# Five norms of a deep hybrid block: the next product's first tile computed ahead of the norm

## The chip, the cores and the metric

The kernel runs on one core of a Trainium2 chip. The metric is the device time of one execution in microseconds (us). The engines are TensorE (PE, with PEld for its weight loads), VectorE (DVE), ScalarE (ACT), GpSimd (POOL) and SyncE (SP), which here issues the DMAs.

## The reference, cut to what matters

The reference computes a deep block on 512 tokens of width 1024: two layers, each of a SwiGLU feed-forward, a mixer and a second feed-forward, and then a second block of attention, RWKV and a feed-forward. Each sublayer begins with the same norm, scaled and shifted by modulation vectors that come from a condition `c`:

```
def rms_norm(x, g):
    xf = x.astype(jnp.float32)
    y = xf * lax.rsqrt(jnp.mean(xf * xf, axis=-1, keepdims=True) + EPS)
    return (y * g.astype(jnp.float32)).astype(x.dtype)

h = rms_norm(x, g) * (1 + scale) + shift
x = x + half * (1 + gate) * sublayer(h)
```

The next product is `h @ W`. Since the root of a token is one number, `h @ W` equals the root of the token times `(x * g * (1 + scale)) @ W`, plus `shift @ W`, which is one row for all tokens. At the end of the second layer there is a norm by `final_g` as well, and the second block's first norm is taken of its result.

## The kernel before

Activations lie transposed: 1024 channels as 8 chunks (`DC`) of 128 partitions, 512 tokens along the free dimension. `K.x` is the residual. Each product is done in three passes to keep float32 precision: the activation is split into `h_hi` and `h_lo`, a weight tile into `w_hi` and `w_lo`, and a chunk contributes `w_hi*h_hi`, `w_hi*h_lo` and `w_lo*h_hi` (L401 to L403), each a large product of 128x128 by 128x512 into one PSUM bank.

`gemm` (L270) runs over the output tiles of a product. A tile of weights is 128 output channels; its 8 chunks make 24 large products. In the projections back to the residual (`project`, L1050) an output block is made of two tiles: 11 chunks each in a feed-forward (33 large products a tile), 8 each in the mLSTM. SP loads raw weights into a ring of 4 slots. ACT makes `w_hi` (`split_hi`, L236) and DVE `w_lo` (`split_lo`, L243) in 2 halves, so the split of tile t+2 waits until tile t is done. The order of each engine's work is written out by hand: in a projection DVE first splits, then updates the residual from the bank (`dve_evac`, L1062), and ACT squares it (`Squares.by_act`, L544); POOL adds up the squares.

A norm lies between a projection and the next product. In `Modulated` (L636) TensorE sums the squares over the channels with one-column products (`sums_pe`, L605), ACT takes the root (L623), DVE the reciprocal (L628), and TensorE spreads it with four 128-column products to a bank with the row of roots for all tokens (`row_of_roots`, L598). Then DVE scales the eight chunks (L665), ACT adds the shift and rounds to `h_hi` (L652), and DVE takes the remainder `h_lo` (L668). Both engines split the weights of tile 1 between the root and the scaling. `first_pair` (L367) runs tiles 0 and 1 together: for each chunk, as it comes, the two products with `h_hi`, and at the end those with `h_lo` (L384).

There are seven such norms behind the first. Five are changed: the hybrid mixer's, that of the feed-forward "f10" (first of layer 1), the mLSTM's, that of "f11" (second of layer 1), and the final head in front of the second block (`FinalModulated`, L873). The final head has two roots: it sums two sets of squares, takes the first root, works out the second from it, and later has POOL multiply `K.x` itself by the first one. The norm behind the hybrid mixer ("f01") and the last in the second block stay as they are.

Behind a norm DVE has other work for each tile done: in the hybrid and the mLSTM four steps of a convolution (L1114, L1117), in f10 the accumulation of modulation vectors (L492, L495) and the gate's product, in f11 only the gate's product, in the second block two steps of a token shift (L2418, L2420).

## Time and profile before

| | |
|---|---|
| median of 3 runs | 3602.83 us (3602.04 to 3604.32) |
| profiled execution | 3600.31 us, span 3598.5 us |
| PE busy | 3466.9 us, 96% |
| DVE busy | 1980.1 us, 55% |
| ACT busy | 1183.8 us, 33% |
| POOL busy | 364.9 us, 10% |
| granted TensorE clock, mean | 0.973 of full speed |

A matmul's span in the profile overlaps that of the next one, so the time of a stream is read from the distances of starts. A clock of 1.00 is 2.4 GHz, 0.50 is 1.2 GHz. An operation's start counts from the beginning of the span. A float32 product of a narrow matrix appears as two instructions.

### The profile page before, as it was taken

The page shows a single profiled execution, that of the slowest core. Times are in us where ns is not written, and L with a number is a line of the kernel's source. Part 1 is how long each engine was busy: PE and PEld are TensorE (multiplying, and loading weights), DVE is VectorE, ACT ScalarE, POOL GpSimd, SP SyncE. Part 2 cuts the span into 40 slices and gives each one's busy share as a digit, 9 for nine tenths or more (in the row PEclk, how much of TensorE's full clock was granted, in tenths as well). Part 3 has the DMA queues.
Part 4 walks back from the last instruction along what each step waited for, and adds up shares of the span by engine and source line. Part 5 has one row for each costly group of instructions (what it writes and reads, how often), then busy time and mean ns, then how long its engine had stood idle before and what let it go on. Part 6 is the DMA issues. An engine that isn't in the chain of part 4 may idle for free. (4 is left out here: it accounts for less than half of the span.)

```text
span 3598.5 us, 56173 instructions
## 1 busy us (share of the span) xinstructions
PE 3466.9 (96%) x22376; PEld 2799.2 (78%) x22376; DVE 1980.1 (55%) x2770; ACT 1183.8 (33%) x1733; POOL 364.9 (10%) x264
## 2 busy tenths in 40 slices
PE   7999999999999999999999999999989999999998
PEld 4888777878888788876678788887768787878886
DVE  6665566756654666465343433355667773454343
ACT  3222245433222322233242322233434542233231
POOL 1000003410000000010101000130103330010000
PEclk9999999999999999999899999999989999989999
DMA  6555322125554555421032223222210002223332
GB/s 248 196 189 178 113 77 73 56 89 189 198 193 138 181 187 202 160 84 50 1 104 95 86 96 109 89 83 84 63 39 6 8 6 71 95 64 98 89 100 70
DMA packets 103764, 382.74 MB, mean 106 GB/s; under 512 B 11424, under 2 KB 15136, under 8 KB 103200
## 3 DMA queue, kind: packets, MB, share of 16 engines
q1 hardware_dynamic: 103584, 380.15, 31.4%
q8 instruction: 136, 2.23, 0.3%
q14 instruction: 44, 0.36, 0.0%
HBM read 378.01 MB, written 2.10 MB: 106 GB/s over the span
## 5 line engine op out<-in xcount | busy, mean ns | idle before, releaser
L401 PE MATMUL bank<-h_hi,w_hi 128*128 128x512 f32 x2616 | 1031.4, 394 | 20.3 <-DVE w_lo L246 17.5
L402 PE MATMUL bank<-h_lo,w_hi 128*128 128x512 f32 x2616 | 1021.8, 391 | 0.0
L403 PE MATMUL bank<-h_hi,w_lo 128*128 128x512 f32 x2616 | 1021.8, 391 | 0.0
L246 DVE TENSOR_TENSOR w_lo<-w_raw,w_hi 128x1024 fp32r<-128x1024 f32 (+2 forms) x480 | 645.9, 1346 | 512.4 <-ACT w_hi L240 502.6
L240 ACT ACTIVATE w_hi<-w_raw 128x1024 fp32r<-128x1024 f32 (+2 forms) x480 | 526.5, 1097 | 345.3 <-PE bank L403 283.5
L401 PEld LDWEIGHTS bank<-h_hi,w_hi 128*128 128x128 f32 x2616 | 493.2, 189 | 138.0 <-DVE w_lo L246 23.3
L403 PEld LDWEIGHTS bank<-h_hi,w_lo 128*128 128x128 f32 x2616 | 493.0, 188 | 104.3
L402 PEld LDWEIGHTS bank<-h_lo,w_hi 128*128 128x128 f32 x2616 | 493.5, 189 | 102.3 <-issue 1.9
L401 PE MATMUL bank<-f_gu_hi,w_hi 128*128 128x512 f32 x704 | 279.4, 397 | 0.0
L403 PE MATMUL bank<-f_gu_hi,w_lo 128*128 128x512 f32 x704 | 279.1, 396 | 0.0
L402 PE MATMUL bank<-f_gu_lo,w_hi 128*128 128x512 f32 x704 | 279.1, 396 | 0.0
L1020 ACT ACTIVATE f_gu_hi<-f_prod_t 128x512 f32 (+1 forms) x88 | 55.6, 632 | 408.0 <-DVE f_prod_t L1027 408.0
L495 DVE SCALAR_TENSOR_TENSOR ada_acc<-ada_tiles,c_act,ada_acc 128x512 f32<-128x512 f32 x210 | 157.5, 750 | 7.2 <-DMA ada_tiles<-in_ada 1.4
L401 PEld LDWEIGHTS bank<-f_gu_hi,w_hi 128*128 128x128 f32 x704 | 132.6, 188 | 32.6
L403 PEld LDWEIGHTS bank<-f_gu_hi,w_lo 128*128 128x128 f32 x704 | 132.6, 188 | 32.4
L402 PEld LDWEIGHTS bank<-f_gu_lo,w_hi 128*128 128x128 f32 x704 | 132.6, 188 | 32.2
L1027 DVE TENSOR_TENSOR f_prod_t<-f_sil_t,bank 128x512 f32<-128x512 f32 x88 | 60.5, 688 | 167.7 <-PE bank L403 167.7
L1017 ACT ACTIVATE f_sil_t<-bank 128x512 f32<-128x512 f32 x88 | 52.7, 599 | 245.7 <-PE bank L403 245.6
L1066 DVE SCALAR_TENSOR_TENSOR residual<-bank,coef,residual 128x512 f32 (+1 forms) x40 | 30.0, 751 | 166.3 <-PE bank L403 166.3
L542 POOL MEMSET sq_acc_f<- 128x512 f32 x5 | 2.6, 526 | 1037.6 <-PE bank L403 1037.6
L1029 DVE TENSOR_TENSOR f_gu_lo<-f_prod_t,f_gu_hi 128x512 f32 (+1 forms) x88 | 60.9, 692 | 77.9 <-ACT f_gu_hi L1020 77.9
L402 PE MATMUL bank<-u_lo,w_hi 128*128 128x512 f32 x256 | 101.5, 396 | 0.0
(618 smaller groups left out, 4604.8 us busy)
## 6 DMA issues: line engine op xcount, KB each, us to landing
ada_tiles<-in_ada SPq DMA_DIRECT2D x180, 512.0 KB, 4.1
w_raw<-in_gu SPq DMA_DIRECT2D x176, 512.0 KB, 4.4
w_raw<-in_dn SPq DMA_DIRECT2D x64, 704.0 KB, 4.2
w_raw<-in_w_ff SPq DMA_DIRECT2D x64, 512.0 KB, 3.6
w_raw<-in_w_hyb SPq DMA_DIRECT2D x36, 512.0 KB, 3.4
w_raw<-in_w_rkv SPq DMA_DIRECT2D x24, 512.0 KB, 3.5
w_raw<-in_w_attn SPq DMA_DIRECT2D x20, 512.0 KB, 3.6
w_raw<-in_w_hout SPq DMA_DIRECT2D x16, 512.0 KB, 3.4
```

The lines of the kernel that those rows point to most:

```text
L240: K.nc.scalar.activation(K.w_hi[:, half, 0:kb * P], K.w_raw[:, slot, 0:kb * P], ACT.Copy).then_inc(K.hi_done.sem, 1)
L246: K.nc.vector.tensor_tensor(K.w_lo[:, half, 0:kb * P], K.w_raw[:, slot, 0:kb * P], K.w_hi[:, half, 0:kb * P].bitcast(F32), ALU.subtract).t ...
L401: nc.tensor.matmul(K.ps[bank][:], wh, hi, start=start, stop=False)
L402: nc.tensor.matmul(K.ps[bank][:], wh, lo, start=False, stop=False)
L403: last_mm = nc.tensor.matmul(K.ps[bank][:], wl, hi, start=False, stop=stop)
L495: ins = v.scalar_tensor_tensor(self.acc[:], block, c, self.acc[:], ALU.mult, ALU.add)
L542: self.K.nc.gpsimd.memset(acc[:], 0.0).then_inc(self.K.sq_added.sem, 1)
L1017: nc.scalar.activation(sil[:, j // 2, :], K.ps[j][:], ACT.Silu).then_inc(sil_done.sem, 1)
L1020: nc.scalar.activation(gu_hi[:, bass.ds(f, 1), :], prod[:, j // 2:j // 2 + 1, :], ACT.Copy).then_inc(guhi_done.sem, 1)
L1027: nc.vector.tensor_tensor(prod[:, j // 2, :], sil[:, j // 2, :], K.ps[j][:], ALU.mult).then_inc(done.sem, 1)
L1029: nc.vector.tensor_tensor(gu_lo[:, bass.ds(f, 1), :], prod[:, j // 2:j // 2 + 1, :], gu_hi[:, bass.ds(f, 1), :].bitcast(F32), ALU.subtract ...
L1066: nc.vector.scalar_tensor_tensor(K.x[:, bass.ds(o, 1), :], K.ps[j // tpo][:, None, :], K.coef[:, bass.ds(o, 1)], K.x[:, bass.ds(o, 1), :], ...
```

## The change

Five norms get `early=True`, and the projection in front of each gets the coming norm as `follow`.

In the projection, each output block of the residual is multiplied by the norm's gain times (1 + scale) as soon as it is updated, and split into `h_hi` and `h_lo`, without the root and the shift: one operation more on ACT (`ahead_act`) and one on DVE (`ahead_dve`) per block. For this the gain is computed at the start of the projection (`gain_ahead`), and the squares' tiles move to memory that the projection's predecessor has left (`vacated`).

In the next product, TensorE runs tile 0 in full at once on these (`early_tile`). Between its 24 large products stand the narrow ones, one at a time (`between`): the 8 sums of squares (16 in the final head), the 4 products of the row of roots (behind the tile in the final head), and 8 new products `shift @ W` of the raw weights with the shift. The true `h` is then made as before, with the scaling of chunk c waiting until the early tile has read it. When it is done, tile 0's bank is copied to memory by ACT, multiplied by the row of roots by DVE, and the shift's column is added by ACT; only then does the tile count as done. Tiles 1 and 2 are run one behind the other with `h_hi`, then with `h_lo` (`next_pair`), instead of tiles 0 and 1 chunk by chunk; the weights of tile 2 are split within the norm (`third_weights`), between chunks 3 and 4 on ACT and between scaling and `h_lo` on DVE. SP holds its loads of later weight tiles until the shift's products are done. Some semaphores are shared with other stages to make room.

```diff
+            if early:
+                sp.wait_ge(K.early_mm.sem, K.early_mm(1))
...
+            def early_tile():
+                pe.wait_ge(K.lo_done.sem, g0 + PRIMED + 1)
+                pe_wait(pe, 0, 0, 0)
+                pe.wait_ge(K.bank_free.sem, K.bank_free(-1))
+                for n in range(3 * kb):
+                    c, part = n // 3, n % 3
+                    hi, lo, bank, start, stop = mm(c, 0)
+                    wh, wl = weights(0, c)
+                    if part == 0:
+                        pe.wait_ge(K.h_ready.sem, K.h_ready(c + 1 - kb))
+                        nc.tensor.matmul(K.ps[bank][:], wh, hi, start=start, stop=False)
+                    elif part == 1:
+                        nc.tensor.matmul(K.ps[bank][:], wh, lo, start=False, stop=False)
+                    else:
+                        nc.tensor.matmul(K.ps[bank][:], wl, hi, start=False, stop=stop).then_inc(K.early_read.sem, 1)
+                    head.between(pe, n)
+                head.behind(pe)
+
+            def next_pair():
+                for j in (1, 2):
+                    pe.wait_ge(K.lo_done.sem, g0 + j + PRIMED + 1)
+                    pe_wait(pe, 0, j, j)
+                    for k in range(kb):
+                        pe.wait_ge(K.h_hi_done.sem, K.h_hi_done(k + 1))
+                        hi, lo, bank, start, stop = mm(k, j)
+                        wh, wl = weights(j, k)
+                        nc.tensor.matmul(K.ps[bank][:], wh, hi, start=start, stop=False)
+                        nc.tensor.matmul(K.ps[bank][:], wl, hi, start=False, stop=False)
+                pe.wait_ge(K.tile_mm.sem, done0 + 1)
+                for j in (1, 2):
+                    for k in range(kb):
+                        hi, lo, bank, start, stop = mm(k, j)
+                        pe.wait_ge(K.h_ready.sem, K.h_ready(k + 1))
+                        last_mm = nc.tensor.matmul(K.ps[bank][:], weights(j, k)[0], lo, start=False, stop=stop)
+                    last_mm.then_inc(K.tile_mm.sem, 1)
...
+    def ahead_act(self, act, o):
+        K.nc.scalar.activation(K.h_hi[:, bass.ds(o, 1), :], K.x[:, bass.ds(o, 1), :], ACT.Identity, scale=K.gain[:, bass.ds(o, 1)]).then_inc(K.h_hi_done.sem, 1)
+    def ahead_dve(self, dve, o):
+        dve.wait_ge(K.h_hi_done.sem, K.h_hi_done(o + 1))
+        K.nc.vector.scalar_tensor_tensor(K.h_lo[:, bass.ds(o, 1), :], K.x[:, bass.ds(o, 1), :], K.gain[:, bass.ds(o, 1)],
+                                         K.h_hi[:, bass.ds(o, 1), :].bitcast(F32), ALU.mult, ALU.subtract).then_inc(K.h_ready.sem, 1)
...
+    def between(self, pe, n):
+        if 2 <= n < 2 + 2 * NT:
+            self.sum_part(pe, n - 2)
+        if 13 <= n < 13 + NT:
+            self.row_part(pe, n - 13)
+        if n >= 2 * DC:
+            self.shift_part(pe, n - 2 * DC)
...
+    def early_act(self, act, second_weights, third_weights):
+        second_weights()
+        self.rms_act(act)
+        for c in range(DC):
+            act.wait_ge(K.scaled.sem, K.scaled(c + 1))
+            K.nc.scalar.activation(K.h_hi[:, c, :], K.t[:, c, :], ACT.Identity, bias=self.shift[:, c:c + 1]).then_inc(K.h_hi_done.sem, 1)
+            if c == 3:
+                third_weights()
+        K.nc.scalar.activation(K.early_tile, self.in_halves(K.ps[0]), ACT.Copy).then_inc(K.early_copied.sem, 1)
+        act.wait_ge(K.early_fixed.sem, K.early_fixed(2))
+        K.nc.scalar.activation(K.ps[0][:], K.ps[0][:], ACT.Identity, bias=K.early_bias[:, 0:1]).then_inc(K.tile_mm.sem, 1)
...
+    def early_dve(self, dve, second_weights, third_weights):
+        second_weights()
+        self.rms_dve(dve)
+        dve.wait_ge(K.rms_row.sem, K.rms_row(1))
+        for c in range(DC):
+            dve.wait_ge(K.early_read.sem, K.early_read(c + 1))
+            v.scalar_tensor_tensor(K.t[:, c, :], K.x[:, c, :], K.gain[:, c:c + 1], K.ps[self.ROW][:], ALU.mult, ALU.mult).then_inc(K.scaled.sem, 1)
+        third_weights()
+        self.bias(dve)
+        for c in range(DC):
+            dve.wait_ge(K.h_hi_done.sem, K.h_hi_done(c + 1))
+            v.scalar_tensor_tensor(K.h_lo[:, c, :], K.t[:, c, :], self.shift[:, c:c + 1], K.h_hi[:, c, :].bitcast(F32),
+                                   ALU.add, ALU.subtract).then_inc(K.h_ready.sem, 1)
+            if c == 1:
+                dve.wait_ge(K.early_copied.sem, K.early_copied(1))
+                v.tensor_tensor(self.in_halves(K.ps[0]), K.early_tile, self.in_halves(K.ps[self.ROW]), ALU.mult).then_inc(K.early_fixed.sem, 1)
...
 class FinalModulated(Modulated):
+    def between(self, pe, n):
+        if 1 <= n < 1 + 4 * NT:
+            self.sum_part(pe, n - 1)
+        if n >= 2 * DC:
+            self.shift_part(pe, n - 2 * DC)
+    def behind(self, pe):
+        self.row_of_roots(pe)
...
         v.reciprocal(K.rs[:], K.rs[:]).then_inc(self.own_r, 1)
+        self.copy_bias(dve)
         dve.wait_ge(self.own_r, 4)
         v.tensor_tensor(K.rs[:], K.rs[:], self.r[:], ALU.mult).then_inc(K.rms_step.sem, 1)
...
+            if follow:
+                follow.ahead_dve(dve, o)
```

## Rows read from the trace of the kernel before

**Rows 1.** The page, busy time of each engine and instructions.
```profile
PE 3466.9 (96%) x22376; PEld 2799.2 (78%) x22376; DVE 1980.1 (55%) x2770; ACT 1183.8 (33%) x1733; POOL 364.9 (10%) x264
```

**Rows 2.** TensorE's waits: us in total, times, longest us.
```profile
PE bank L401 <- DVE w_lo L246: 18.8, 22, 4.5
```

**Rows 3.** Windows, five norms: us; busy PE, PEld, DVE, ACT, POOL; clock; DMA.
```profile
411.29:433.16 21.87, 18.55 (x82) 14.85 (x80) 14.30 (x23) 9.27 (x14) 0.00 (x0) 0.77 0.31 100
1168.93:1190.80 21.87, 18.56 (x83) 14.80 (x81) 14.34 (x23) 9.52 (x14) 0.00 (x0) 0.77 0.20 73
1544.44:1566.28 21.84, 18.53 (x82) 14.84 (x80) 15.27 (x25) 9.52 (x14) 8.39 (x7) 0.77 0.27 89
1983.10:2003.81 20.71, 16.75 (x75) 13.51 (x73) 14.12 (x21) 9.52 (x14) 0.00 (x0) 0.84 0.08 26
2355.89:2378.73 22.84, 19.84 (x99) 16.89 (x97) 15.09 (x28) 10.71 (x17) 6.89 (x3) 0.85 0.16 47
```

**Rows 4.** Windows in and behind the hybrid's norm.
```profile
418.99:424.00 5.01, 5.01 (x12) 3.95 (x13) 5.01 (x9) 4.46 (x7) 0.00 (x0) 0.50 0.22 86
...
433.16:444.30 11.14, 11.14 (x49) 9.19 (x50) 10.50 (x14) 2.73 (x5) 0.00 (x0) 1.00 0.29 94
```

**Rows 5.** Timeline of the hybrid's norm: start, us, engine, line, operation.
```profile
411.73 0.75 DVE L1066 SCALAR_TENSOR_TENSOR residual<-bank,coef,residual 128x512 f32<-128x512 f32 x1 [4.01 <-PE bank L403]
...
412.51 0.63 ACT L547 ACTIVATE sq_f<-residual 128x512 f32<-128x512 f32 x1 [5.88 <-DVE residual L1066]
...
413.19 1.38 PE L617 MATMUL bank<-consts,sq_f 128*128 128x1 f32 x8 [0.33 <-ACT sq_f L547]
414.61 0.26 ACT L623 ACTIVATE rms_rs<-bank,cols 128x4 f32<-128x4 f32 x1 [1.47 <-PE bank L617]
414.77 1.05 ACT L240 ACTIVATE w_hi<-w_raw 128x1024 fp32r<-128x1024 f32 x1
...
415.14 2.07 PE L602 MATMUL bank<-consts,rms_rs 128*128 128x128 f32 x8 [0.57 <-DVE rms_rs L628]
...
417.34 5.36 DVE L665 SCALAR_TENSOR_TENSOR h_scaled<-residual,gain,bank 128x512 f32<-128x512 f32 x8 [0.26 <-PE bank L602]
418.12 5.33 ACT L652 ACTIVATE h_hi<-h_scaled,mods 128x512 fp32r<-128x512 f32 x8 [2.30 <-DVE h_scaled L665]
...
418.99 0.77 PE L378 MATMUL bank<-h_hi,w_hi 128*128 128x512 f32 x1 [1.77 <-ACT h_hi L652]
...
422.61 5.38 DVE L668 SCALAR_TENSOR_TENSOR h_lo<-h_scaled,mods,h_hi 128x512 fp32r<-128x512 f32 x8
```

**Rows 6.** Timeline of TensorE, a batch of narrow products between large ones.
```profile
712.70 1.84 PE L1618 MATMUL bank<-consts,ssd_acc 128*128 128x1 f32 x16
714.40 0.47 PE L401 MATMUL bank<-hyb_hi,w_hi 128*128 128x512 f32 x1
```

**Rows 7.** Timeline of DVE behind the hybrid's norm.
```profile
435.99 1.22 DVE L246 TENSOR_TENSOR w_lo<-w_raw,w_hi 128x1024 fp32r<-128x1024 f32 x1
437.13 0.55 DVE L1114 TENSOR_SCALAR proj<-conv_raw,cols 128x512 f32<-128x512 f32 x1
...
439.95 0.54 DVE L1114 TENSOR_SCALAR proj<-conv_raw,cols 128x512 f32<-128x512 f32 x1
```

**Rows 8.** Timeline of DVE behind the norm of f10.
```profile
1191.17 2.39 DVE L495 SCALAR_TENSOR_TENSOR ada_acc<-ada_tiles,c_turn,ada_acc 128x512 f32<-128x512 f32 x3
...
1199.44 0.75 DVE L495 SCALAR_TENSOR_TENSOR ada_acc<-ada_tiles,c_turn,ada_acc 128x512 f32<-128x512 f32 x1 [1.30 <-DMA ada_tiles<-in_ada]
```

**Rows 9.** Timeline of DVE in a feed-forward's and the mLSTM's projection.
```profile
1156.62 2.10 DVE L246 TENSOR_TENSOR w_lo<-w_raw,w_hi 128x1408 fp32r<-128x1408 f32 x1 [0.53 <-ACT w_hi L240]
...
1974.69 1.47 DVE L246 TENSOR_TENSOR w_lo<-w_raw,w_hi 128x1024 fp32r<-128x1024 f32 x1 [1.65 <-ACT w_hi L240]
```

**Rows 10.** Timeline of DVE in the final head.
```profile
2362.60 0.16 DVE L911 TENSOR_TENSOR rms_rs<-rms_rs,final_r 128x4 f32<-128x4 f32 x1
...
2365.00 5.36 DVE L665 SCALAR_TENSOR_TENSOR h_scaled<-residual,gain,bank 128x512 f32<-128x512 f32 x8 [0.37 <-PE bank L602]
```

More of the change, by code:

```diff
@@ L278, in gemm @@
     done0 = g0 + PRIMED
+    early = head and head.early
     with one_block(K) as block:
@@ L316, in body @@
                     if head and isinstance(i, int) and t < 3:
-                        if t < 2:
+                        if t < 2 and not (early and t == 0):
                             split_hi(K, act, kb, (t + 2) % RING, t % SPLIT, g0 + t + 2)
@@ L343, in body @@
                     if head and isinstance(i, int) and t < 3:
-                        if t < 2:
+                        if t < 2 and not (early and t == 0):
                             split_lo(K, dve, kb, (t + 2) % RING, t % SPLIT, g0 + t + 2)
@@ L362, in _ @@
         def _(pe):
-            if head:
+            if head and not early:
                 head.pe(pe)
@@ L389, in body @@
                     t = turn * i + j
-                    if head and isinstance(i, int) and t < 2:
+                    if early and isinstance(i, int) and t < 3:
+                        if t == 0:
+                            early_tile()
+                        if t == 1:
+                            next_pair()
+                    elif head and isinstance(i, int) and t < 2:
                         if t == 0:
@@ L588 @@
     SUM, ROW = 4, 5
+    early = False
     def __init__(self, K):
@@ L636, with __init__, gain_ahead @@
 class Modulated(Rms):
-    def __init__(self, K, gain, scale, shift):
+    SHIFT_BANK = 6
+    def __init__(self, K, gain, scale, shift, early=False):
         super().__init__(K)
-        self.gain, self.scale, self.shift = gain, scale, shift
+        self.gain, self.scale, self.shift, self.early = gain, scale, shift, early
+    def gain_ahead(self, dve):
+        K = self.K
+        dve.wait_ge(K.x_written.sem, K.x_written(0))
+        K.nc.vector.scalar_tensor_tensor(K.gain[:], self.scale, 1.0, self.gain, ALU.add, ALU.mult).then_inc(K.x_written.sem, 1)
+        dve.wait_ge(K.x_written.sem, K.x_written(1))
@@ new lines, in ahead_advance, with sum_part @@
+    def ahead_advance(self):
+        K = self.K
+        K.x_written.base += self.GAIN_STEPS
+        K.h_hi_done.base += DC
+        K.h_ready.base += DC
+    def sum_part(self, pe, i):
+        K, mm = self.K, self.K.nc.tensor.matmul
+        total, half = K.ps[self.SUM], NT * len(K.sq_parts)
+        a, t = i % half, i % NT
+        acc, end = K.sq_parts[a // NT]
+        if i == 0:
+            pe.wait_ge(K.sq_added.sem, K.sq_added(0))
+        if i == half:
+            pe.wait_ge(K.sq_done.sem, K.sq_done(0))
+        last = mm(total[:, a:a + 1], (acc if i < half else end)[:, t * P:(t + 1) * P], K.ones[:, 0:1], start=i == 0, stop=i >= half, skip_group_check=True)
+        if i == 2 * half - 1:
+            last.then_inc(K.rms_sum.sem, 1)
@@ new lines, in row_part, with shift_part @@
+    def row_part(self, pe, t):
+        K = self.K
+        if t == 0:
+            pe.wait_ge(K.rms_step.sem, K.rms_step(1))
+        last = K.nc.tensor.matmul(K.ps[self.ROW][:, t * P:(t + 1) * P], K.rs[:, t:t + 1].to_broadcast([P, P]), K.ident, start=True, stop=True)
+        if t == NT - 1:
+            last.then_inc(K.rms_row.sem, 1)
+    def shift_part(self, pe, c):
+        K = self.K
+        last = K.nc.tensor.matmul(K.ps[self.SHIFT_BANK][:, 0:1], K.w_raw[:, 0, c * P:(c + 1) * P], self.shift[:, c:c + 1], start=c == 0, stop=c == DC - 1)
+        if c == DC - 1:
+            last.then_inc(K.early_mm.sem, 1)
@@ L672, in advance @@
         self.rms_advance()
-        self.K.x_written.base += 1
+        if self.early:
+            for c, n in ((self.K.early_mm, 1), (self.K.early_read, DC), (self.K.early_copied, 1), (self.K.early_fixed, 2)):
+                c.base += n
+        else:
+            self.K.x_written.base += 1
         for c in (self.K.scaled, self.K.h_hi_done, self.K.h_ready):
@@ L878, in __init__ @@
     def __init__(self, K, gain, scale, shift, final, row):
-        super().__init__(K, gain, scale, shift)
+        super().__init__(K, gain, scale, shift, early=True)
         self.final, self.row = final, row
@@ L882, in __init__, with bias, gain_ahead, behind @@
         self.r, self.both = K.final_small
-    def pe(self, pe):
+    GAIN_STEPS = 2
+    def between(self, pe, n):
[3 more added lines that the diff above has]
+            self.shift_part(pe, n - 2 * DC)
+    def bias(self, dve):
+        pass
+    def gain_ahead(self, dve):
+        super().gain_ahead(dve)
+        K = self.K
+        K.nc.vector.tensor_tensor(K.gain[:], K.gain[:], self.final, ALU.mult).then_inc(K.x_written.sem, 1)
+        dve.wait_ge(K.x_written.sem, K.x_written(2))
+    def behind(self, pe):
         K, mm = self.K, self.K.nc.tensor.matmul
-        self.rms_pe(pe)
+        self.row_of_roots(pe)
         for t in range(NT):
@@ L1047, in root_table, with project @@
     K.nc.scalar.activation(K.pad4[:], K.consts[:, 0:NT], ACT.Sqrt)
-def project(K, w, kb, tpo, mm, nxt, gate, half, squares, turn=4, side=None, ready=None):
+def project(K, w, kb, tpo, mm, nxt, gate, half, squares, turn=4, side=None, ready=None, follow=None):
     nc = K.nc
@@ L2185, in ml_heads, with final_head, second_block @@
     return out, N["spr"].sem
-def second_block(K):
+def final_head(K):
+    row = K.at("final_row", [P, S], F32, K.arena + 100 * 1024)
+    return FinalModulated(K, col(K, "mix_pre", 0, 8), K.mods[:, 152:160], K.mods[:, 144:152], col(K, "final_g", 0, 8), row)
+def second_block(K, head):
     nc, d = K.nc, K.dram
@@ L3527, in build @@
                 with stage(K):
-                    mlstm(K, nxt, head, gate)
+                    mlstm(K, nxt, head, gate, follow)
             else:
```

116 lines of the change are left out of this document (81 added, 35 removed).

## The prediction

> **What bounds the kernel now.** I read the page first: TensorE is busy for 96% of the span [rows 1], so time can only be saved where its stream of large products breaks or slows. The list of TensorE's waits came next: the largest sum is 18.8 us in 22 short waits for a weight's remainder `w_lo`, no more than 4.5 us at a place [rows 2]; no steady stage is starved. Then I laid one window over each norm that changes, from the start of the projection's last large product to the start of the third tile (tile 2) of the next product: 21.87, 21.87, 21.84, 20.71 and 22.84 us [rows 3]. Two tiles are done in each, 48 large products. A full-speed stretch shows 11.14 us for 48 of them, 0.232 each [rows 4]. So the five windows hold 109.1 us where 55.7 us would do: some 53 us are all that the change can touch, in the order hybrid, FFN 10, mLSTM, FFN 11, final head. Last I read the timeline of the first of them engine by engine [rows 5]. It is a chain: residual update 411.73, square 412.51, sums 413.19, root 414.61, row of roots 415.14, scaling 417.34, `h_hi` 418.12, first large product 418.99. The granted clock is at its half level (1.2 GHz) from inside the gap until 424.0, and products there take 0.42 us [rows 4].
>
> **Part by part: the early tile.** I walk the hybrid's norm on the profile's clock. The last large product starts at 411.29, the modulation's narrow products stay, and the early tile starts at 411.80. ACT does the last square at 412.51; the last chunk's early `h_hi` starts at 413.05, its `h_lo` on DVE at 413.79 (a back-to-back ACT operation follows after 0.54 to 0.66, a dependent one after 0.78) [rows 5]. The tile needs that chunk only in its 22nd product, so it doesn't wait.
>
> **The narrow products.** A float32 narrow product is two instructions. In a batch between large ones 16 of them take 712.70 to 714.40, 0.106 each [rows 6], so 0.213 a product. No row shows one singly between large products. Bounds: nothing (its loads hide behind the large one) and 0.43 (the half-clock pitch of the rows of roots, 2.07 us for 8 instructions) [rows 5]. I take 0.213, since the batch is the nearest row: one load hides, two don't.
> The Trainium skill (TensorE: Matmul & The Clock Gate, "What happens when you issue a matmul") says that the queue pulls weight loads ahead of matmuls in flight. By it alone the single products would be nearly free; the batch's 0.106 an instruction doesn't show that.
> Eight sums then stand between products 2 to 9, each pair 0.44, and end at 415.6 instead of 414.3. ACT's root goes to about 415.95, the reciprocal to 416.25; DVE has by then done the split of tile 1, which moved ahead of the root. TensorE takes the four row products from 416.7 to 418.2. The scaling starts at 418.55, 1.2 us LATER than the 417.34 of before. The eight shift products (new, 1.7 us) and the rest of the tile end at 421.55.
>
> **Behind it.** DVE is now the long queue. Scaling takes 5.27 us (417.34 to 422.61) [rows 5], to 423.8; the split of tile 2, newly put here, 1.14 (435.99 to 437.13) [rows 7]; the bias copy 0.2; eight `h_lo` 5.28 (0.66 each); the product with the row of roots in the bank 0.69: to 431.1. ACT fits in: four `h_hi`, the split of tile 2 (1.05, as the row of tile 1 [rows 5]), four more to 425.7, the bank's copy, the bias, to about 427.9. TensorE does tiles 1 and 2 from 421.6, waits some 1 us for `h_hi` behind the inserted split, and ends both at 433.5, at full clock.
> Tile 3 needs a split on DVE, and behind `h_lo` stands the work of the tiles already done. In the hybrid that is 2.8 to 2.9 us of convolution a tile (437.13 to 439.95) [rows 7]: evacuation 0 to 434.0, split to 435.2, evacuations 1 and 2 to 440.85, split of tile 4 to 442.1. Tile 4 starts at 442.2. Before it starts at 433.16 + 11.14 = 444.3. **Hybrid: 2.1 us won**, not the 7.5 us gap. The mLSTM's norm has the same convolution and 21.84 for 21.87: **2.1**.
> FFN 10 has four modulation steps there, 2.9 us (2.39 for three); tile 4 waits for the modulation's data, whose load is issued behind the fourth step (ending at 1193.5) and is first used at 1199.44 [rows 8]. That step ends 24.5 us after the last large product before, 22.7 in the new walk: **1.9**.
> FFN 11 has no such work, so TensorE sets the end. Before, tile 3 starts 20.71 + 5.57 = 26.3 us after the last large product; new, without the 0.3 us of modulation's narrow products, 434.3 - 411.3 - 0.3 = 22.7: **3.6**.
> The final head has 16 sums, between products 1 to 16. They end at about 2363.2; 2.3 us later than before. Then DVE copies the bias in the middle of the chain of roots, and this waits for the last shift product, that is for the end of the early tile: 2366.7. The roots step ends at 2367.3, where it began at 2362.60, and scaling starts at 2368.5 instead of 2365.00 [rows 10]. TensorE idles 0.7 and 1.0 us around the rows. Tile 3 starts at 2384.6, before at 2378.73 + 5.57 = 2384.3: **0.3 lost**.
>
> **The projections ahead.** Each output block gets one ACT operation (0.65) and one on DVE (0.75), some 40 of each. They stand before the split of the weights of the tile after next. In the mLSTM's projection, the shortest tile (24 products, 5.6 us), the split of `w_lo` runs from 1974.69 to 1976.16 [rows 9], and is wanted at 1977.5. Put 0.67 later, and less slowed by the squares' addition beside it, it ends at about 1976.8. In the FFN's the split of before ends at 1158.7 [rows 9]; the early `h_lo` and two modulation steps move it to at most 1160.3, with the tile boundary at 1161.2. So nothing is paid. If the cover goes: up to 0.7 us an output, 8 outputs, five projections, 28 us; I hold nearly all of it off.
> The gain's column moves to the projection's start (0.2 us on DVE, under a tile of 7.7 us), the cleared accumulators wait for a semaphore long up, both zero. SP now holds the loads of tiles 4 and 5 until the early tile's shift products are done (421.5 instead of 412.85 and 417): they land some 4 us later, and tile 4 is split no earlier than 434. SP's modulation loads stand behind the same wait but are due later. Zero; without the cover, a tile's load of 4 us.
>
> **Sum.** 2.1 + 1.9 + 2.1 + 3.6 - 0.3 = 9.4 us. The profiled execution took 3600.31 us (span 3598.5), which gives 3590.9; it stands 2.5 under the median of the runs, 3602.83, so the forecast is **3593.5**. The bounds of the narrow price move the scaling by about 1.0 us earlier (then ACT's and DVE's splits hold the root) or 2.6 us later, in four norms, three of them bound by DVE: 3589.5 (1.0 in four) to 3604 (2.6 in four).
>
> **Rivals.**
> A. The single narrow products are nearly free, and the final head's chain is hardly later than now. The pitch in [rows 6] speaks against. Scaling 1.0 us earlier in four norms, and about 1.5 in the head: 3593.5 - 5.5 = 3588.
> B. The queue on DVE (scaling, split, `h_lo`, evacuations) eats the whole early tile, or the added operations in the projections cost 0.2 us a block where a split ran close. Against: the slack worked out above, for: DVE's unbroken run of splits and evacuations, of the kind in [rows 7], with some 20 us of work ahead of it. 9.4 less about 8: 3601.5.
> C, the other side. The granted clock drops during the early tile, because every second instruction is narrow. For it: it fell in all five windows (means 0.77 to 0.85) [rows 3], while sums and rows ran. Against: large products pass in between in at least half of that time. Price: products at 0.42 instead of 0.232 over some 7 to 10 us (18 products, 3.4 us), the narrow ones at 0.43 push the scaling by 1.5 or more; 4.9 us in four norms, DVE's queue not hiding it: 3593.5 + 20 = 3613. It decides from about half of the norms on. In the head alone, where TensorE idles twice, a half clock would cost up to 2 us; that is in my range.
>
> **Chances.** Forecast 0.58, A 0.14, B 0.18, C 0.10. A change under 0.2% (7.2 us) can't be told from none. The forecast's own range, 3589.5 to 3597.5, is faster by over 0.2% in about 0.8 of its part; with A that makes 0.60 faster; B and the rest 0.29 same; C and a little of B 0.11 slower. Range: 3586 to 3604.
>
> **What would show it.** Right: the first large product of the next weights starts about 0.5 us behind the last of the projection; scaling in the hybrid starts 7.3 us behind that last product (6.05 now); granted clock 1.00 through the first four windows; last product to tile 4's start 30.9 us in the hybrid (33.0 now), FFN 11 to tile 3 22.7 (26.3 now), the head unchanged. The single narrow product's price can be read as the pitch of large ones around it less 0.232. Wrong: half clock inside the windows (C), `w_lo` waits inside the projections (B), pitches near 0.24 around narrow ones (A).

## The result, with the profile after

The changed kernel took 3579.07 us (median of four runs, 3575.18 to 3582.20), the kernel before 3603.57 beside it (3602.04 to 3608.23): ratio 0.9929, 95% interval 0.9912 to 0.9947. Gained are 24.5 us; 9.4 were forecast (3593.5 us), and the time lies under the range, 3586 to 3604. The profiled execution took 3580.06 us with a span of 3578.2, that is 20.3 less than the span of before.

The page's busy line [rows 1 of before], then the longest sum of TensorE's waits [rows 2]:

```profile
PE 3448.2 (96%) x22456; PEld 2780.9 (78%) x22456; DVE 2018.7 (56%) x2820; ACT 1212.7 (34%) x1783; POOL 360.7 (10%) x264
```
```profile
PE bank L457 <- DVE w_lo L252: 27.8, 28, 4.5
```

TensorE has 80 instructions more and is busy 18.7 us less: what it won is speed, not only gaps. The waits for `w_lo` rose from 18.8 to 27.8 us, so part of each norm's gain turned into that wait. Windows of the changed kernel over the same five places, from the last large product to the 49th behind it (the start of the third tile before; in the changed kernel the same amount of work is done by then, but tiles 1 and 2 both lack products), columns as in [rows 3]:

```profile
410.82:427.62 16.80, 16.80 (x98) 13.47 (x97) 12.33 (x20) 9.82 (x16) 0.00 (x0) 1.00 0.46 161
1166.49:1183.29 16.80, 16.80 (x99) 13.46 (x97) 12.34 (x20) 9.84 (x16) 0.00 (x0) 1.00 0.26 96
1538.76:1555.56 16.80, 16.80 (x99) 13.46 (x97) 12.74 (x22) 9.83 (x16) 7.62 (x7) 1.00 0.41 147
1964.33:1980.74 16.41, 16.41 (x91) 13.38 (x89) 12.24 (x19) 9.84 (x16) 0.00 (x0) 1.00 0.27 96
2333.16:2355.22 22.06, 20.12 (x114) 15.98 (x113) 12.97 (x24) 10.83 (x18) 0.00 (x0) 1.00 0.22 69
```

TensorE is busy from end to end in four of them, and the granted clock is 1.00 in all. Against 109.1 us of before they take 88.9, so 20.2 us are won at this point. More than half of that is given back on DVE. Its timeline behind the hybrid's norm (start, us, line, operation; answers to [rows 5] and [rows 7]):

```profile
418.28 5.36 DVE L799 SCALAR_TENSOR_TENSOR h_scaled<-residual,gain,bank 128x512 f32<-128x512 f32 x8 [2.16 <-PE bank L747]
423.55 1.22 DVE L252 TENSOR_TENSOR w_lo<-w_raw,w_hi 128x1024 fp32r<-128x1024 f32 x1
...
426.68 4.06 DVE L804 SCALAR_TENSOR_TENSOR h_lo<-h_scaled,mods,h_hi 128x512 fp32r<-128x512 f32 x6
...
430.80 0.55 DVE L1312 TENSOR_SCALAR proj<-conv_raw,cols 128x512 f32<-128x512 f32 x1
431.38 2.33 DVE L1315 SCALAR_TENSOR_TENSOR proj<-conv_raw,cols,proj 128x512 f32<-128x512 f32 x3
433.62 1.22 DVE L252 TENSOR_TENSOR w_lo<-w_raw,w_hi 128x1024 fp32r<-128x1024 f32 x1
...
440.39 1.22 DVE L252 TENSOR_TENSOR w_lo<-w_raw,w_hi 128x1024 fp32r<-128x1024 f32 x1
```

From 423.55 on DVE hardly rests, and tile 4 of the weights (the fifth) waits for the split of 440.39: it starts at 441.67, 30.85 us behind the last large product, where 30.9 were forecast.

The distances from a projection's last large product to the start of tile 3 and of tile 4, worked out from the starts of products in each trace:

```
                hybrid      FFN 10      mLSTM       FFN 11      head
before          27.47/32.91 27.46/33.33 27.46/32.90 26.28/31.72 28.42/33.86
after           24.07/30.85 23.93/30.75 23.92/30.78 22.66/28.26 29.10/35.33
saved, tile 4   2.06        2.58        2.12        3.46        -1.47
```

That is 8.75 us. Where the rest of the span's 20.3 lies: start to the first norm 0.5; stretches between norms -0.1, 0.7 and 0.5; behind the head -1.0; **from the mLSTM's norm to FFN 11's 11.0**. Nearly all of these 11.0 are in the mLSTM's four heads, whose instructions the change doesn't touch. Windows from one head's denominators (20 one-column products) to the next's, three periods, first of the kernel before, then of the changed one:

```profile
1678.80:1712.90 34.10, 33.29 (x142) 22.75 (x142) 11.14 (x29) 9.22 (x22) 5.49 (x7) 0.90 0.00 0
1712.90:1747.00 34.10, 33.31 (x143) 22.70 (x143) 14.43 (x34) 10.50 (x23) 5.50 (x7) 0.90 0.00 1
1747.00:1781.10 34.10, 33.32 (x143) 22.65 (x143) 14.43 (x34) 10.50 (x23) 5.50 (x7) 0.90 0.00 0
```
```profile
1671.70:1704.10 32.40, 31.65 (x142) 21.27 (x142) 11.11 (x29) 9.21 (x22) 5.49 (x7) 0.95 0.00 1
1704.10:1734.90 30.80, 29.99 (x143) 20.58 (x143) 14.45 (x34) 10.50 (x23) 5.50 (x7) 1.00 0.00 1
1734.90:1765.60 30.70, 29.92 (x143) 20.50 (x143) 14.36 (x34) 10.50 (x23) 5.50 (x7) 1.00 0.00 1
```

The same instructions; the granted clock is 0.90 in the one and, from the second head on, 1.00 in the other. Before, it fell to half (1.2 GHz) in each head. TensorE waits 0.8 us for the exponentials (`mlh_e`; 2.2 in the first head), runs 20 one-column products, and the large ones behind them start at half clock. The two rows and a window of the kernel before:

```profile
1678.84 3.31 PE L1962 MATMUL bank<-consts,mlh_e 128*128 128x1 f32 x20 [2.16 <-DVE mlh_e L2122]
...
1712.91 3.25 PE L1962 MATMUL bank<-consts,mlh_e 128*128 128x1 f32 x20 [0.78 <-DVE mlh_e L2122]
```
```profile
1714.20:1721.00 6.80, 6.80 (x19) 4.75 (x20) 3.48 (x9) 0.33 (x1) 0.00 (x0) 0.50 0.01 4
```

One such fall costs 3.4 us a head (34.1 for 30.7). A run of heads that take 34.1 us each is called stuck below, one of heads at 30.7 free.

### The profile page after: what moved, and what is told of

Same layout as the page of the kernel before. It is cut to its first block and busy times, and to the rows that moved or that the text cites. A ratio compares the mean times of both kernels' runs of the same rounds, so it can differ in the third digit from the quotient of the medians.

```text
span 3578.2 us, 56582 instructions
## 1 busy us (share of the span) xinstructions
PE 3448.2 (96%) x22456; PEld 2780.9 (78%) x22456; DVE 2018.7 (56%) x2820; ACT 1212.7 (34%) x1783; POOL 360.7 (10%) x264
## 3 DMA queue, kind: packets, MB, share of 16 engines
q1 hardware_dynamic: 103584, 380.15, 30.7%
## 5 line engine op out<-in xcount | busy, mean ns | idle before, releaser
L457 PE MATMUL bank<-h_hi,w_hi 128*128 128x512 f32 x2576 | 1015.5, 394 | 29.2 <-DVE w_lo L252 26.5
L459 PE MATMUL bank<-h_hi,w_lo 128*128 128x512 f32 x2576 | 1005.6, 390 | 0.0
L458 PE MATMUL bank<-h_lo,w_hi 128*128 128x512 f32 x2576 | 1005.3, 390 | 0.0
L252 DVE TENSOR_TENSOR w_lo<-w_raw,w_hi 128x1024 fp32r<-128x1024 f32 (+2 forms) x480 | 634.3, 1321 | 397.7 <-ACT w_hi L246 386.5
L457 PEld LDWEIGHTS bank<-h_hi,w_hi 128*128 128x128 f32 x2576 | 485.3, 188 | 146.5 <-DVE w_lo L252 30.0
L459 PEld LDWEIGHTS bank<-h_hi,w_lo 128*128 128x128 f32 x2576 | 485.0, 188 | 102.4
L458 PEld LDWEIGHTS bank<-h_lo,w_hi 128*128 128x128 f32 x2576 | 485.5, 188 | 100.7 <-issue 1.9
L457 PEld LDWEIGHTS bank<-f_gu_hi,w_hi 128*128 128x128 f32 x704 | 132.2, 188 | 32.4
L459 PE MATMUL bank<-u_hi,w_lo 128*128 128x512 f32 x256 | 100.9, 394 | 0.0
```

The source lines that it names most:

```text
L252: K.nc.vector.tensor_tensor(K.w_lo[:, half, 0:kb * P], K.w_raw[:, slot, 0:kb * P], K.w_hi[:, half, 0:kb * P].bitcast(F32), ALU.subtract).t ...
L457: nc.tensor.matmul(K.ps[bank][:], wh, hi, start=start, stop=False)
L458: nc.tensor.matmul(K.ps[bank][:], wh, lo, start=False, stop=False)
L459: last_mm = nc.tensor.matmul(K.ps[bank][:], wl, hi, start=False, stop=stop)
```

## The experiments

All but three single executions were timed beside the kernel before. Three questions: is it the clock in the heads, what decides it, and are the norms' terms right.

**Are the kernels' times one group?** The kernel before again, no edit.

> The kernel before, unchanged, for a second trace. Theory H (the changed kernel won some 11 us in the mLSTM heads only because its heads meet the clock's steps at another offset, each head's pause no longer falling to the half clock): the half clock appears in all four heads again, as in the first trace (five stretches of 6.8 us between 1680 and 1806), and the time is 3602 to 3608. If the offset were drawn anew in each execution, the number of half-clock stretches in the heads would differ from the first trace and single times would scatter by some 10 us. Rival R (the shared semaphores or the shorter code of the heads make them faster): the same time, nothing said on the clock.

Measured: 3606.05 us (3593.42 to 3608.98, 10 runs), ratio 0.9997 (0.9983 to 1.0011). Heads 34.08 a period, as before. The distances of the norms in its trace are those of before to 0.3 us.

**Do shared semaphores hold the heads?** The change let `mlh_` counts share the hybrid's semaphores; this edit does that alone.

```
-    N = {n: K.count("mlh_" + n) for n in names}
+    N = {n: Count(K.hybrid_then_ml[n]) if n in K.hybrid_then_ml else K.count("mlh_" + n) for n in names}
```

> The kernel before with only the change's sharing of six semaphores between the hybrid mixer and the mLSTM heads. Rival R: the heads go from about 200 us to 189 us, total about 3592. Theory H: within 2 us of the kernel before, 3602 to 3606, half clock in all heads.

Measured: 3606.62 us (3598.16 to 3610.02), ratio 1.0004 (0.9991 to 1.0017), heads unchanged. The rival is refuted.

**Does the moment of arrival decide?** N idle large products into a bank that nobody reads, in the mLSTM's projection, ahead of the heads: 13, 6, then 4.

```
+    def pads(pe, t):
+        if isinstance(t, int) and t == 12:
+            for n in range(4):
+                nc.tensor.matmul(K.ps[6][:], K.h_hi[:, 0, 0:P], K.h_hi[:, 0, :], start=True, stop=True)
```

> The kernel before with 13 idle large products (3.0 us) on TensorE behind the 13th tile of the mLSTM's up product, ahead of the heads. Their results go to a bank that nobody reads. [...] Theory H: the heads fall to the half clock less often, some 11 us less in them, total 3603.6 + 3.0 - 11 = 3596. Rival R: 3603.6 + 3.0 = 3606.6.

> The same with 6 idle products (1.4 us). Theory H: the heads take some time between that of the kernel before and 11 us less, and it goes with the number of half-clock stretches in them at about 3.3 us a stretch of 6.8; total 3594 to 3605. Rival R: 3605.0, heads as before.

> The kernel before with 4 idle large products (0.9 us) on TensorE ahead of the mLSTM heads. In five traces of kernels of the kind before, the first head began 1.6 to 2.2 us behind a step of the clock where nothing was added; this makes it 2.5 to 3.1. Theory H2: that is among the free offsets (2.98 with 6 products was free): period of the heads 30.7 us, not 34.1, and most times lower by some 9 us: median about 3597. Rival R: no effect of an idle product, 3607 and heads of 34.1 us.

Measured: 13: 3605.20 us (3598.74 to 3611.74), where 3596 were expected; the profiled execution had heads of 34.09 a period. 6: 3605.53 us, five runs at 3598.1 to 3602.7 and five at 3608.4 to 3611.5; its profiled execution is of the lower five and has free heads (30.73). Neither moved the median (ratios 0.9996 and 1.0007). 4: **3596.07 us** (3592.86 to 3600.09, 10 runs), ratio 0.9970 (0.9961 to 0.9980): 0.9 us of useless work made the kernel before 11.1 us faster than the 3607.21 beside it. The three periods with 4:

```profile
1678.80:1712.80 34.00, 33.23 (x142) 22.89 (x142) 11.13 (x29) 9.22 (x22) 5.50 (x7) 0.90 0.00 0
1712.80:1743.50 30.70, 29.95 (x142) 20.54 (x142) 14.37 (x34) 10.51 (x23) 5.50 (x7) 1.00 0.00 1
1743.50:1774.30 30.80, 29.97 (x143) 20.55 (x143) 14.47 (x34) 10.51 (x23) 5.50 (x7) 1.00 0.00 1
```

From the second head on the clock stays full, as in the changed kernel. So the 11 us belong to no instruction of the change: they can be had without it.

**The changed kernel again.** Unaltered on two chips, and with 4 and 8 idle products.

> The changed kernel, unchanged, for a second trace and more times. Theory H2 (as H, with a cause for the offset: in the kernel before each norm ends inside a half-clock stretch, and its end moves only about half as far as its beginning against the clock's steps, so that seven norms pull all executions to nearly the same offset at the heads, mostly one in which each head falls; with the norms at full clock nothing pulls any more, and the heads are met at all offsets): the time scatters in two groups, about 3576 to 3585 with the heads free and about 3588 to 3598 with them at half clock, more in the first; median 3580 to 3590 against 3606 before. Rival R2 (the heads are freed by the change itself, always): all times within 3575 to 3584.

> The changed kernel unaltered, on another chip. If the offset at the heads decides and the changed kernel reaches them at more than one offset, its times spread from about 3577 to 3596, the heads in its trace 237 to 239 us where the profiled execution is of the faster part and 245 or more where it is of the slower; median 3584 to 3590, 15 to 20 us under the kernel before.

> The changed kernel with 4 idle large products (0.9 us) on TensorE ahead of the mLSTM heads, as before_pad4 had them. In three traces of the changed kernel the first head began 0.86 to 1.00 us behind a step of the clock, and the heads were free. Theory H2: 1.8 us is among the offsets at which each head falls (1.64 to 2.15 did): heads at a period of 34.1 us, times about 3595 to 3599, so the same idle products that took 11 us from the kernel before now add 10 in those executions that were fast. Rival (TensorE's idle products help in themselves, say by their activity): 3583 or less.

> The same with 8 idle products (1.8 us). Theory H2: 2.7 to 2.8 us, among the free offsets (2.57 to 2.98 were): period 30.7 us in the trace, few or no times in the slow group; median 3584 to 3588, under the 3593.9 that the changed kernel gave in the last call. Rival as above: nothing more than the 4 products gave.

Measured: again 3593.88 us (3581.85 to 3596.10, 7 runs), ratio 0.9960 (0.9946 to 0.9974); third 3583.66 (3581.50 to 3593.64, 6 runs), 0.9946 (0.9929 to 0.9962); pad 4 3591.73 (3581.50 to 3593.78, 4 runs); pad 8 3582.30 (3580.04 to 3591.68, 4 runs). The same 4 idle products that freed the heads of the kernel before left those of the changed kernel stuck in its trace (34.09), and 8 left them free (30.73): it is not the added work as such that helps. The changed kernel, unaltered, has two groups: of its 17 executions 11 took 3575.2 to 3586.3 us (mean 3581.7) and 6 took 3593.4 to 3596.1 (mean 3594.3), none between. The third's profiled execution is of the upper group, and has the half clock in its heads:

```profile
1672.20:1704.60 32.40, 31.64 (x142) 21.45 (x142) 11.11 (x29) 9.22 (x22) 5.50 (x7) 0.95 0.00 1
1704.60:1738.70 34.10, 33.29 (x142) 22.76 (x142) 14.43 (x34) 10.50 (x23) 5.50 (x7) 0.90 0.00 1
...
```

The moments at which the granted clock changes in a trace all stand on one even grid. The offset of a head is its start less the last point of that grid. Where the pauses were left as they are, the second and third heads that took 34.1 us began at offsets of 1.48 to 2.18 us, and those that took 30.7 at 2.24 to 2.90, whichever kernel it was (16 traces, those of the later experiments included). There is a third form: heads of 32.4 us, with half as long a stretch of half clock, at 1.46, 1.47 and 3.17. So in these traces the offset alone tells what a head takes. Two heads of the third form, from the kernel with the plain head below:

```profile
1707.80:1740.20 32.40, 31.63 (x142) 21.48 (x142) 14.37 (x34) 10.51 (x23) 5.50 (x7) 0.95 0.00 1
1740.20:1772.60 32.40, 31.64 (x142) 21.38 (x142) 14.38 (x34) 10.51 (x23) 5.50 (x7) 0.95 0.00 1
```

A period of 34.1 us carries a head to nearly the same offset again (2.15, 2.10, 2.03, 1.98 in the kernel before), and so does one of 30.7 (2.71, 2.72, 2.73 in the changed one). That is why an execution mostly stays as it began. It need not: the offset of stuck heads falls by 0.03 to 0.07 us a head, and one trace (narrow products in batches, below) went from 1.49 to 1.46 and so to 32.4.

**Parts of the change.** Without FFN 11's early tile; without the hybrid's.

```
-            elif step != "hyb":
+            elif step not in ("hyb", "ml"):      # the other kernel: ("hyb", "f00")
```

> The changed kernel with the norm of f11 alone as before. It lies behind the heads. From the last large product of the mLSTM's projection to the start of tile 3: 26.3 us instead of the 22.4 or so of the changed kernel, the half clock back in this norm, everything else unchanged: 3.6 us to 3.9 us more there. Rival to the walk (the early tile's worth is not that of the norm but of the clock behind it): under 2 us.

> The changed kernel with the hybrid mixer's norm alone as before. From the last large product to the start of tile 4: 33.0 us instead of 30.85, 2.1 us more; the half clock back in this norm. Theory H2: the heads take 237 or 248 us as the offset falls, which one run can't foretell.

Measured: 3586.76 us and 3596.74 (one run each). In the traces FFN 11's distance to tile 3 goes to 26.13 (3.5 more, 3.6 to 3.9 expected) and to tile 4 to 31.57 (3.3 more), the hybrid's to tile 4 to 32.98 (2.1 more); the others stay within 0.2. So these two norms pay for themselves. The second kernel's heads were stuck (34.1): its 3596.74 tells of that and not of the hybrid.

**The head as before, with 8 idle products**, meant as a better kernel, since the early tile had cost 1.5 us there.

```
-    super().__init__(K, gain, scale, shift, early=True)
+    super().__init__(K, gain, scale, shift)
```

> The candidate: the changed kernel with the 8 idle products, and the final head's norm as before, since it measured 1.5 us later at tile 4 with the change. Last large product to the start of tile 4 33.9 us there instead of 35.3. By that 1.5 us under after_pad8: 3583 to 3587. Rival: the final head's new order also keeps the clock up behind it; then no gain or a loss of up to 3 us.

Measured: 3596.66 us (3586.86 to 3603.28, 10 runs), ratio 0.9972. It failed, for two reasons that its trace shows. The mLSTM's heads took 34.1, 32.4 and 32.4 us, against 34.1, 30.7 and 30.7 in the trace with 8 idle products and the early head. And the plain head took 37.59 us to tile 4, the early one 35.33. With the early head the distance is 35.32 to 35.34 in all eleven traces. With the plain one it is 33.86 and 33.76 in the two traces of the unedited kernel before and 35.98 to 37.59 in all seven traces of kernels that have an edit elsewhere. So the early head loses 1.5 us against the unedited kernel, and gains 0.7 to 2.3 against the edited ones. Why an edit elsewhere changes the plain head isn't shown; how it does stands in the last section.

**Narrow products in batches.** All eight sums behind the sixth large product, four rows behind another, the shifts behind the last.

```
-        if 2 <= n < 2 + 2 * NT:
-            self.sum_part(pe, n - 2)
+        if n == 5:
+            for i in range(2 * NT):
+                self.sum_part(pe, i)
```

> The changed kernel with its narrow products in batches in four norms (8 sums behind the 6th large product, 4 rows behind the 14th, 8 shift products behind the last) instead of one at a time; the final head stays. By the walk a narrow product costs 0.213 us between large ones either way (measured 0.225 singly): last large product of the projection to the start of tile 4 in the hybrid's norm 30.85 us, within 0.5. Rival (singly is what makes it work: batches let the clock drop or wait on the chain): over 1 us later, half clock in the norm.

> The changed kernel with its narrow products in batches again: eight sums behind one large product, four row products behind another, eight shifts behind a third. Theory (a lone narrow product costs 0.22 us of TensorE, one within a batch 0.11): tiles 3 come 0.7 us earlier in the hybrid, mLSTM and f11 norms, tile 4 0.46 later in f10; about 1.7 us faster than the changed kernel, lost in the two groups of times, so between 3578 and 3592. Rival (singly is better, since the large products hide them): 2 to 4 us slower.

Timelines of the hybrid's early tile, TensorE, first singly, then in batches:

```profile
412.14 0.28 PE L739 MATMUL bank<-consts,sq_acc_f 128*128 128x1 f32 x2
412.27 0.48 PE L412 MATMUL bank<-h_hi,w_hi 128*128 128x512 f32 x1
412.59 0.28 PE L739 MATMUL bank<-consts,sq_acc_f 128*128 128x1 f32 x2
...
415.33 0.28 PE L739 MATMUL bank<-consts,sq_f 128*128 128x1 f32 x2
415.47 0.48 PE L414 MATMUL bank<-h_lo,w_hi 128*128 128x512 f32 x1
...
421.39 0.48 PE L428 MATMUL bank<-h_hi,w_hi 128*128 128x512 f32 x1
```
```profile
411.62 0.95 PE L739 MATMUL bank<-consts,sq_acc_f 128*128 128x1 f32 x8
412.43 1.03 PE L739 MATMUL bank<-consts,sq_f 128*128 128x1 f32 x8
413.32 0.49 PE L412 MATMUL bank<-h_hi,w_hi 128*128 128x512 f32 x1
...
420.15 0.49 PE L428 MATMUL bank<-h_hi,w_hi 128*128 128x512 f32 x1
```

Singly a narrow product costs 412.59 - 412.14 - 0.232 = 0.22 us, in the batch (413.32 - 411.62) / 8 = 0.21. (The 0.11 of the second expectation is the price of one of its two instructions, and wrong for a product.) The tile takes as long either way: 10.06 and 10.03 us. But the batch's last sum starts 3.0 us behind the tile's start, and the single ones' 4.0, so scaling starts 6.75 us behind the last large product and not 7.46. Tiles 3 come 0.7 us earlier. Time: 3584.91 us (3578.99 to 3593.81, 6 runs) and 3585.78 (one run). A gain of 1.7 us can't be seen between groups that stand 12 us apart; by the traces batches are the better form.

**Work in the heads' pauses.** Seven idle large products between the denominators of each head, then eighteen, in both kernels.

```
                         last = mm(K.ps[4][:, t:t + 1], e_of(sb, (t - sb) * P, P), K.ones[:, 0:1], start=sb == 0, stop=sb == t)
+                        if (t, sb) != (3, 3):
+                            for _ in range(2): mm(K.ps[5][:], K.h_hi[:, 0, 0:P], K.h_hi[:, 0, :], start=True, stop=True)
```

> The kernel before with seven idle large products per head between the narrow den products of the mLSTM heads (into a bank that nobody reads). Theory (the half clock in the heads' pauses makes the two groups of times): the granted clock stays 1.00 in the heads, a head takes 30.73 us plus 7 x 0.227 = 1.6, so 32.3 us and not 34.1, the four heads take about 3.4 x 4 less and 6.4 us more; time about 3598 and one narrow group. Rival (something else makes them): 6.4 us slower than the kernel before, about 3612, with two groups 10 us apart as before.

> The changed kernel with the same seven idle products per head. Theory: one narrow group, about 3588; against before_fill 9 to 10 us faster, which is what the norms alone save (8.9 us by their distances in the traces), and not 24. Rival (the change itself saves the time in the heads): the distance to before_fill stays near 20 us, and after_fill is 6.4 us slower than the changed kernel.

> The kernel before with eighteen idle large products per head, two behind each narrow den product but the last. Theory (the half clock belongs to the pause with little work): no half clock in the heads, period 30.73 + 18 x 0.233 = 34.9 us, heads 4.2 x 4 = 16.8 us longer than the free ones and 3.4 longer than the stuck ones; about 3609. Rival (the waits ahead of the den products alone, some 1 us, pull the clock down whatever follows): half clock as before in some heads, 38 us for such a head, 3615 and more.

> The changed kernel with the same eighteen. Theory: the heads as in before_full to 0.5 us, time about 3599, 9 to 10 us under before_full. Rival (a part of the gain lies in the rest of the kernel): 14 to 16 us under before_full, as between the kernels with seven.

Measured with seven: 3607.70 (3597.77 to 3615.44) and 3592.05 (3586.05 to 3596.00), 12 runs each. The clock still fell in the first and third pause of both traces (periods 37.2, 32.4, 35.6 and 35.7, 32.4, 35.7): the remedy was too weak. The changed kernel's times closed to one group of 10 us, the other's still spread over 18. With eighteen: 3616.44 (3612.74 to 3623.99, 6 runs) and 3602.83 (3599.84 to 3607.95, 12 runs). The first two periods with eighteen, kernel before, then changed:

```profile
1678.20:1717.90 39.70, 38.92 (x161) 27.72 (x161) 11.18 (x29) 9.23 (x22) 5.50 (x7) 0.87 0.00 0
1717.90:1752.80 34.90, 34.12 (x161) 23.93 (x161) 14.40 (x34) 10.51 (x23) 5.50 (x7) 1.00 0.00 1
...
```
```profile
1676.20:1715.90 39.70, 38.95 (x160) 27.45 (x160) 11.11 (x29) 9.22 (x22) 5.49 (x7) 0.87 0.00 1
1715.90:1750.80 34.90, 34.13 (x160) 23.94 (x160) 14.39 (x34) 10.51 (x23) 5.50 (x7) 1.00 0.00 1
...
```

From the second head on the clock is full in both, and the period is the 34.9 us worked out ahead; the first head fell, after its longer wait. The heads are now the same in both kernels (109.5 us for three periods), and what is left between them is 13.6 us; with seven it is 15.7. Each has about 6 us of uncertainty (from the intervals of the ratios).

**Putting it together.** Mean over the traces of each kind, the norms' distances to tile 4 add up to 166.0 us before (eight traces) and 156.0 after (seven with all five early tiles and single narrow products): 1.7, 2.0, 1.9, 4.0 and 0.3, **9.9 us**. In the unedited kernels alone they are 164.7 (two traces) and 156.1 (three), 8.5 us; the head makes most of the difference. The stretches ahead of and between the norms, without that of the mLSTM's heads, give 1.3 more (2.1 in the unedited kernels). A part of the heads' gain is there in either state: the first head took 34.1 us in the unedited kernel before and 32.4 in the changed one, stuck or free behind it, and the stretch from the mLSTM's norm to FFN 11's is 405.8 and 405.9 us in the two traces of the kernel before and 404.4 in the stuck one of the changed kernel. That is another 1.4. Together it makes 12.0 to 12.6. With eighteen products in the pauses the heads are alike, the 1.4 doesn't count, and 11.2 stand against 13.6.

Within a group it is much the same: of all 114 executions of the kernel before 17 lie under 3600 (mean 3595.1), 13.5 above the changed one's lower group, and 97 over it (mean 3606.2), 11.8 above its upper group. The rest of the gain is the mix: 15% of executions in the lower group before, 65% after. The means (3604.5 and 3586.1) stand 18.4 us apart: 12.5 within the groups and 6 by the mix. The first measurement, 24.5, had four executions of the lower group against four of the upper. No unedited execution of the kernel before in its lower group was traced; that its heads run free there is inferred from the traces with 4 and 6 idle products.

**Open.** The offset of the first head was 1.67 to 2.15 us in four of five traces of the kernel before without idle products ahead of the heads (0.11 in the fifth); behind an unfilled pause that leaves the second head stuck. In six such traces with the early norms it was 0.48 to 1.21. Of those six the two with filled pauses don't bear on the next step; in the other four the first head took 32.4 us and brought the second to 2.18 (stuck) once and to 2.57 to 2.71 (free) three times. The two traces with batches stand outside this: their first heads began at 3.31 and 1.55, and the second was stuck in both. Why each kernel arrives where it does is not shown, and the theory of the expectation for the changed kernel's repeat, that half-clock norms pull all executions to one offset, was not tested. Without the hybrid's early tile the first head began at 0.02 and the second stuck; without FFN 11's, which comes behind the heads, nothing changed there. That agrees with arrival as the cause and proves no rule. The stretch from the head's tile 4 to the end varied from 1207.1 to 1215.2 us over all traces, with no difference between the kinds (1211.1 and 1210.7 in the mean).

## Why the prediction failed, by its own steps

- *"some 53 us are all that the change can touch"*: **this is the step that failed.** It took every stretch outside the five windows to keep its time. The heads' stretch became 11.0 us shorter although no instruction there changed, because their pauses let the clock fall to half or not by the moment at which they begin (offsets of 1.48 to 2.18 and of 2.24 to 2.90 us), and every norm ahead of them had moved that moment. No rival had it: C looked for a half clock inside the early tile only. The trace of before held the sign, equal periods of 34.1 us with a granted clock of 0.90 in a stage whose pause is 0.8 us, and I did not open it, since the diff doesn't touch it.
- *The early tile.* Right: 411.33 for 411.80 forecast, 0.51 us behind the last large product; granted clock 1.00 in the first four windows, and in the fifth too. Rival C did not happen in any trace.
- *Narrow products at 0.213 each.* Measured 0.22 singly. Rival A is refuted: nothing of them hides. The Trainium skill (TensorE: Matmul & The Clock Gate, "What happens when you issue a matmul") has weight loads pulled ahead; by this timeline that did not make them free. The scaling started 7.46 us behind the last large product, forecast 7.3. The reason given, that one load hides and two don't, no run tested.
- *Hybrid 2.1, mLSTM 2.1.* Measured 2.06 and 2.12, with DVE's evacuations as the end of the chain, as walked. FFN 10: forecast 1.9, measured 2.58 (2.04 in the mean of the traces). FFN 11: 3.6 to tile 3, measured 3.62.
- *Head 0.3 lost.* Measured 0.68 lost to tile 3 and 1.47 to tile 4. The scaling came as forecast (12.7 us behind the last large product for 12.6), but I had ended the walk with TensorE; in the trace DVE is late. Its rows in the changed head:

```profile
2354.21 4.06 DVE L804 SCALAR_TENSOR_TENSOR h_lo<-h_scaled,mods,h_hi 128x512 fp32r<-128x512 f32 x6
...
2358.33 1.64 DVE L2624 TENSOR_TENSOR lora<-shift_raw 128x512 f32<-128x512 f32 x1
2360.01 1.06 DVE L2626 SCALAR_TENSOR_TENSOR lora<-lora,cols,shift_raw 128x512 f32<-128x512 f32 x1
2361.00 1.21 DVE L252 TENSOR_TENSOR w_lo<-w_raw,w_hi 128x1024 fp32r<-128x1024 f32 x1
```

  The first tile's token shift (1.64 and 1.06 us) stands ahead of the split of 2361.00, which tile 3 waits for: tile 3 starts at 2362.26, and that split ends 29.1 us behind the last large product. Before, the split of tile 3 also stood behind one token shift, but it ended 26.7 us behind that product, 1.7 us ahead of need, because `h_lo` was done 5.3 us earlier in that count.
- *Projections ahead: no cost.* Right: the stretches with the projections in them took no longer (342.2 us before and 341.5 after ahead of the mLSTM's norm, 341.1 and 340.6 ahead of the head).
- *The sum.* 9.4 forecast, 8.75 in the pair of traces and 9.9 in the mean over all: the sum held, partly by luck, since FFN 10 gave 0.7 more in the pair and the head took 1.2 more. Rival B (DVE eats the whole gain) is refuted as a case, though DVE gave back more than half: 20.2 us at the 49th large product, 8.75 at tile 4.
- *The median forecast* was worked out from one execution of the kernel before. Both have two groups some 12 us apart, wider than the whole gain forecast; the three runs shown (3602.04 to 3604.32) did not tell of the lower one.

## What to carry to other kernels

A stretch that a change only shifts in time isn't safe from it: look in the trace of before for stages with a short pause in each turn, a granted clock just under 1 and equal periods, and put their two levels (here 34.1 and 30.7 us a head) into the range. Before crediting a change with what it gained, delay the kernel before by about a microsecond, by several amounts, and time that too; here 0.9 us gave 11 us, and 1.4 and 3.0 us gave nothing in the median. Where an engine's idle time is filled, walk the next engine to the end of its queue, since here more than half of the gain was paid back there (20.2 us to 8.75). And finish the chain's narrow products in a batch early rather than spread over the tile: here they cost the same (0.21 and 0.22 us each) and the scaling came 0.7 us sooner.

## What the runs showed of the hardware

- Half clock can hold on to a stage from turn to turn: 34.08, 34.07, 34.08 us per head in one execution, 30.73 in another of the same instructions, decided by less than 0.1 us of the second head's offset (2.18 stuck, 2.24 free). Seven large products among a pause's narrow ones didn't keep the clock up, eighteen did, but not behind the wait of 2.2 us.
- DVE and POOL slow one another, and which of them pays is not fixed by the instructions. In the plain head of the unedited kernel before (two traces) eight `h_lo` took 5.38 us on DVE while POOL's first residual operation took 5.07. In all seven traces of kernels with an edit elsewhere POOL took 1.76 and DVE 8.30, though POOL began 1.46 us behind DVE in both, and tile 4 came 2.1 to 3.8 us later. Whether it goes by the kernel or by the execution, one or two traces of each can't tell. The row of one of the seven (kernel with shared semaphores):

```profile
2370.35 8.30 DVE L668 SCALAR_TENSOR_TENSOR h_lo<-h_scaled,mods,h_hi 128x512 fp32r<-128x512 f32 x8
```
